# Three-layer fp32 kernel: mLSTM values and the joined local values and gates computed with tokens as the stationary operand

## Chip, cores and metric

One core of one Trainium2 chip runs the whole program. The metric is device time in microseconds (us) of one execution; a time given for a kernel is the median of its runs.

## The reference

The program is two layers of one kind and then one of another, on 512 tokens (S) of width 1024. In each of the first two layers a normalised x is projected, mixed by two branches, projected back and followed by an MLP:

```
h = rmsnorm(x, norm_mix_g[l]);  proj = h @ w_in
mqk, mv, mo, mi, mf, aq, ak, av, ga, gb = split(proj)   # widths 1024 1024 1024 4 4 1024 256 256 1024 1024
mq, mk = split(silu(causal_conv(mqk)));  mv: 4 heads of 256
hm = mlstm(mq, mk, mv, ig = mi + b, logf = log_sigmoid(mf + b))  # normalised, * sigmoid(mo)
ha = sliding_window_attention(aq, ak, av)                  # 16 query heads of 64, 4 key/value heads
x += (sigmoid(ga) * (hm @ w_branch_m) + sigmoid(gb) * (ha @ w_branch_a)) @ w_out
x += square(relu(rmsnorm(x) @ w_up)) @ w_down
```

The change touches `mv` (the mLSTM's values, four heads of 256), `av` (the window attention's "local" values, 256 wide) and the gates `mi`, `mf` (4 each). The third layer (an NSA layer with three attention branches and 48 gate columns) is touched only in how its gate weights are held.

## The kernel before

**Number format.** Every large product is made of three fp32r matmuls: high part by high part, low by high, high by low. ScalarE rounds a weight tile to its high part `w_hi`, GpSimd subtracts to get `w_lo`, and the activations have a high and a low part too: `hx` from x times the gain alone (not yet normalised), `hT` from the normalised x.

**Units.** Weights come in *units* of 128 output columns by 1024 inputs (512 KB), loaded by SP into a two-deep ring `w_raw`, split by ScalarE and GpSimd. A unit is 24 matmuls of 512 columns on TensorE, given in four quarters `u0 h0 m1 u1` of six (function `quarter`): the weights are the stationary operand, the 512 tokens move, and the result lies feature-major (features on partitions) in PSUM bank 0 or 1. A layer has 140 units. In all three layers TensorE's order is written out by hand as lists of steps, and every engine walks the same lists:

```
PRE_TAIL = unit("v", 0) + unit("v", 1) + [("TK", 0)] + CONV[0:2] + [("TK", 1)] + CONV[2:3] + [("gatesT",)]
PRE_FIRST = unit("k", 0) + unit("k", 1)[:3] + [("norm_",)] + unit("k", 1)[3:] + [("gates",)] + PRE_TAIL
loop_turn: [begin] + CONV[done:] + unit("conv", 1) + unit("mv", 0) + unit("mv", 1)
           + [("TV", 0)] + unit("q", 0) + [("TV", 1), ("bc",)] + unit("q", 1) + place_fill([("ST", 0), ...
```

**The stretch ahead of the loop (PRE).** Keys `k` come from `hx`, so TensorE can start before the norm is known. `norm_` sums the squares over partitions with a matmul against ones, ScalarE makes `rs` (the reciprocal root) of it (`norm`, L1191, L1193), and VectorE multiplies results by it later (`store`, L1676). `gates` (`gate_gemm`, L692 to L694) multiplies a full 128-column unit of gate weights, padded from 8 columns, with 24 matmuls of 512 columns. Then come two units of local values `v`; since attention wants them token-major, VectorE scales them into `vtmp` and TensorE transposes them in groups of four 128x128 tiles (`TK`, helper `heads4`, L681). Meanwhile VectorE makes the eight tiles of the normalised x (`tile`, L1802), ScalarE their high parts (L1224), VectorE their low parts (`tile_lo`, L1796), and VectorE and ScalarE work on four-partition rows of the gates (`gate_rows_in`, `gate_rows`, `gate_rows_max`, L1842 to L1857). `gatesT` (L739) transposes these rows. `conv 0` is the first unit on `hT`.

**The loop.** Four turns, one for each head. A turn has units conv 0 and 1 (queries and keys of the mLSTM head), `mv` 0 and 1 (its values), q 0 and 1, six gate units, and between their quarters the small matmuls of both attentions: `bc`, `ST` (scores), `NUM` (values times scores, with `vbuf` as the moving operand) and the window's steps. The `mv` result is feature-major as well: ScalarE copies it to `vtmp`, TensorE transposes it (`TV`, `heads4`), ScalarE copies it to `vbuf`.

**Elsewhere.** `head_values` (L653 to L655) already computes the third layer's values the other way: the 128x128 tile of tokens is stationary and 512 columns of weights move, so that the result comes token-major in four banks.

## Time and profile before

| | |
|---|---|
| median of 3 runs | 2216.64 us (2215.83 to 2217.93) |
| the profiled execution's own time | 2215.26 us |
| its span in the trace | 2213.5 us |
| instructions | 31354 |
| TensorE busy (matmuls) | 2170.8 us, 10211 matmuls |
| VectorE, ScalarE, GpSimd busy | 1047.5, 1085.4, 974.4 us |
| mean granted TensorE clock | 0.996 |
| DMA | 198.70 MB, mean 90 GB/s |

The busy times are sums of modelled durations with overlaps taken out. A matmul's record is longer than the distance to the next one, because successive matmuls are pipelined; what a matmul costs on TensorE is the distance between the starts of two neighbours.

### The profile page before, as it was taken

To read this page: it belongs to the slowest core of one execution; us is meant where nothing else is said; L and a number is where in the kernel's file an instruction comes from. 1 tells how busy PE (TensorE), PEld (TensorE's weight loads), DVE (VectorE), ACT (ScalarE), POOL (GpSimd) and SP (SyncE) were. 2 spreads that over 40 slices of the span, in tenths; PEclk is the share of its full clock that TensorE was granted. 3 is DMA by queue.
4 is the path that set the end of the run, shared out by engine and by line. 5 is a ranking of instruction groups with operands and counts; after the bars stand their busy time and mean duration, and the time that the engine had idled before them with its cause. 6 is when DMAs were issued, how large, how long until landed. Compare 5 with 4: busy or idle time off the path is not lost.

```text
span 2213.5 us, 31354 instructions
## 1 busy us (share of the span) xinstructions
PE 2170.8 (98%) x10211; PEld 1790.0 (81%) x10211; DVE 1047.5 (47%) x2197; ACT 1085.4 (49%) x2267; POOL 974.4 (44%) x757
## 2 busy tenths in 40 slices
PE   7999999999999999999999999999999999999998
PEld 6888888888888888888888788888888787778766
DVE  7356355533132234563563723322324736767773
ACT  6456466434232234464564724322324427787783
POOL 3333333444444444433333344544444435555544
PEclk9999999999999999999999999999999999999999
DMA  4222222223232222222222232322222431221203
GB/s 141 77 86 77 86 86 67 86 95 105 98 102 93 97 95 95 86 77 77 88 75 86 67 104 99 102 95 95 95 95 95 165 124 58 77 67 49 77 29 124
DMA packets 60287, 198.70 MB, mean 90 GB/s; under 512 B 6814, under 2 KB 13519, under 8 KB 59536
## 3 DMA queue, kind: packets, MB, share of 16 engines
q1 hardware_dynamic: 54128, 184.43, 25.4%
q10 hardware_dynamic: 6048, 12.84, 1.6%
q8 instruction: 64, 1.05, 0.2%
q14 instruction: 47, 0.39, 0.1%
HBM read 192.99 MB, written 4.26 MB: 89 GB/s over the span
## 4 chain that ended last, share of the span: by engine, by line
issue 57%; POOL 26%; PE 10%; DVE 5%; ACT 1%; POOLq 1%; DMA 0%; DVEq 0%; ACTq 0%
POOL w_lo L546 26%; PE ps L644 2%; PE ps L646 2%; PE ps L645 2%; DVE Pn L2268 1%; PE ps L1008 1%; PE ps L999 1%; PE ps L1021 1%; DVE PTn L2284 1%; POOLq L542 1%; PE ps L1022 1%; POOLq L544 1%; DVE ocur L2297 0%; DVE y L2255 0%; DVE sz L1733 0%
## 5 line engine op out<-in xcount | busy, mean ns | idle before, releaser
L546 POOL TENSOR_TENSOR w_lo<-w_raw,w_hi 128x512 fp32r<-128x512 f32 x592 | 780.8, 1326 | 1048.8 <-ACT w_hi L1088 1046.2
L644 PE MATMUL ps<-hT_hi,w_hi 128*128 128x512 f32 x1568 | 631.8, 403 | 1.7 <-DVE hT_lo L1796 1.1
L1088 ACT ACTIVATE w_hi<-w_raw 128x512 fp32r<-128x512 f32 x664 | 412.1, 627 | 421.6 <-PE ps L646 373.5
L646 PE MATMUL ps<-hT_hi,w_lo 128*128 128x512 f32 x1568 | 614.4, 392 | 0.0
L645 PE MATMUL ps<-hT_lo,w_hi 128*128 128x512 f32 x1568 | 613.4, 391 | 0.0
L646 PEld LDWEIGHTS ps<-hT_hi,w_lo 128*128 128x128 f32 x1568 | 295.5, 188 | 64.4
L644 PEld LDWEIGHTS ps<-hT_hi,w_hi 128*128 128x128 f32 x1568 | 296.0, 189 | 60.9 <-issue 2.4
L645 PEld LDWEIGHTS ps<-hT_lo,w_hi 128*128 128x128 f32 x1568 | 296.3, 189 | 56.4 <-issue 0.5
L644 PE MATMUL ps<-u_hi,w_hi 128*128 128x512 f32 x512 | 199.2, 389 | 0.0
L645 PE MATMUL ps<-u_lo,w_hi 128*128 128x512 f32 x512 | 199.2, 389 | 0.0
L646 PE MATMUL ps<-u_hi,w_lo 128*128 128x512 f32 x512 | 199.2, 389 | 0.0
L1768 DVE TENSOR_TENSOR x<-x,ps 128x512 f32<-128x512 f32 x64 | 44.0, 687 | 256.2 <-PE ps L646 256.2
L560 POOL TENSOR_TENSOR w_lo<-w_raw,w_hi 128x512 fp32r<-128x512 f32 x72 | 93.0, 1295 | 116.9 <-ACT w_hi L1088 116.9
L1740 DVE SCALAR_TENSOR_TENSOR e_buf<-ps,rs 128x512 f32<-128x512 f32 x64 | 44.3, 692 | 208.6 <-PE ps L646 208.6
L1141 ACT ACTIVATE u_hi<-e_buf 128x512 fp32r<-128x512 f32 x64 | 40.5, 633 | 172.9 <-DVE e_buf L1740 172.9
L644 PEld LDWEIGHTS ps<-u_hi,w_hi 128*128 128x128 f32 x512 | 96.1, 188 | 20.0
L646 PEld LDWEIGHTS ps<-u_hi,w_lo 128*128 128x128 f32 x512 | 96.1, 188 | 20.0
L645 PEld LDWEIGHTS ps<-u_lo,w_hi 128*128 128x128 f32 x512 | 96.1, 188 | 19.8
L1703 DVE SCALAR_TENSOR_TENSOR aq<-ps,aq 64x512 fp32r<-64x512 f32 x32 | 22.0, 689 | 149.7 <-ACT aq L1113 149.2
L1574 ACT ACTIVATE Pn<-Pn,st 128x128 f32<-128x128 f32 (+3 forms) x128 | 71.6, 560 | 25.2 <-DVE st L2268 25.1
L2268 DVE CUSTOM_DVE_ANT_0 Pn<-ps,biasn 128x128 f32<-128x128 f32 (+3 forms) x128 | 60.3, 489 | 24.9 <-DVEq L1649 24.5
L1392 ACT ACTIVATE Pw<-L,st 128x257 f32<-128x257 f32 (+1 forms) x128 | 60.9, 477 | 22.4 <-DVE st L2020 20.0
(339 smaller groups left out, 3489.7 us busy)
## 6 DMA issues: line engine op xcount, KB each, us to landing
w_raw<-w_all SPq DMA_DIRECT2D x332, 512.0 KB, 3.3
bias<-scr_w ACTq DMA_DIRECT2D x8, 512.0 KB, 3.7
biasn<-scr_n SPq DMA_DIRECT2D x4, 1024.0 KB, 5.7
w1k<-w_in ACTq DMA_DIRECT2D x2, 1024.0 KB, 7.2
w1v<-w_in ACTq DMA_DIRECT2D x1, 2048.0 KB, 12.6
scr_x<-x ACTq DMA_DIRECT2D x1, 2048.0 KB, 7.2
x<-scr_x SPq DMA_DIRECT2D x1, 2048.0 KB, 8.1
out<-x SPq DMA_DIRECT2D x16, 128.0 KB, 1.8
```

What stands on the lines that cost most here:

```text
L546: nc.gpsimd.tensor_tensor(w_lo[:, h, :], raw[:, h // 2, (h % 2) * HALF:(h % 2 + 1) * HALF], w_hi[:, h, :].bitcast(F32), ALU.subtract).then ...
L560: nc.gpsimd.tensor_tensor(w_lo[:, 2 * u.b + h, :], raw[:, u.b, h * HALF:(h + 1) * HALF], w_hi[:, 2 * u.b + h, :].bitcast(F32), ALU.subtrac ...
L644: nc.tensor.matmul(ps[:, p, :], wh, hi[:, kk, :], start=(kk == 0), stop=False)
L645: nc.tensor.matmul(ps[:, p, :], wh, lo[:, kk, :], start=False, stop=False)
L646: last = nc.tensor.matmul(ps[:, p, :], wl, hi[:, kk, :], start=False, stop=(kk == KT - 1))
L1088: nc.scalar.activation(w_hi[:, 2 * p + h, :], raw[:, p, h * HALF:(h + 1) * HALF], ACT.Copy)\
L1141: nc.scalar.activation(u_hl[0][:, n, :], e_buf[:, e.b, :], ACT.Square).then_inc(u_hi_done, 1)
L1392: nc.scalar.activation(Pw[:, qt % 2, hd, W0 - 1:W0 + n], L[:, hd, W0 - 1:W0 + n], ACT.Exp, scale=-1.0, bias=st[:, 0, j:j + 1], accum_out=s ...
L1574: nc.scalar.activation(p_, p_, ACT.Exp, scale=-1.0, bias=st[:, 0, j:j + 1], accum_out=st[:, 1, j:j + 1]).then_inc(probs, 1)
L1740: V.scalar_tensor_tensor(e_buf[:, e.b, :], g, 0.0, rs[:, :], ALU.max, ALU.mult).then_inc(g_free[u.b], 1)
L1768: V.tensor_tensor(x[:, n, :], x[:, n, :], g, ALU.add).then_inc(g_free[u.b], 1)
L2268: last = V.tensor_tensor_reduce(out=Pn[:, qt % 2, hd, 0:n], in0=ps[:, 2 + b_, e * n:(e + 1) * n], in1=reverse(biasn, hd, n), scale=1.0, sc ...
```

## The change

1. **Local values and gates together (`vg`).** The 256 columns of `av` and the 8 of the gates are one weight matrix of 264 columns (VW), in buffers of its own (`gv_hi`, `gv_lo`, `gv_raw`), loaded in two halves and split outside the ring. `group_values` computes them token-major: for each of the 8 input tiles k and 4 token tiles, the token tile of `hx` is stationary and 264 columns move. Results lie in four banks (2 to 5). ScalarE copies them out, scaled by the token's norm factor as a per-partition scalar (`group_out`). The units `v`, the product `gates` and the transposes `TK` go.
2. **The norm factor as a column.** Beside the matmul of `norm_`, step `norm0` has four matmuls of one column that give the sums token by token; two ScalarE instructions make `rs_tok` of them.
3. **The gate rows.** The gates are now token-major, so `GT` transposes them to rows (eight transposes of 128x4). VectorE's `gate_rows_in` has three instructions in place of four and comes behind all tiles of the normalised x.
4. **Values of heads 0 and 1 (`mx`).** Four units, in PRE, from `hx` (unnormalised), through `head_values`, token-major in banks 0 to 3; ScalarE scales by `rs_tok` on the way to two buffers `vbuf` (`first_pair_out`, eight copies).
5. **Values of heads 2 and 3 (`mv`).** Four units in turn 2 of the loop, from `hT`, the same way in banks 2 to 5 (`second_pair_out`). The other turns have no value units, and no turn has the transposes `TV`.
6. **Moves.** The tables' matmuls go between `mx` 1 and `mx` 2; `gatesT` between `mx` 2 and `mx` 3. The third layer's gate weights have 48 columns instead of 128. Units of a layer: 138.

The core of the diff:

```diff
-PRE_TAIL = (unit("v", 0) + unit("v", 1) + [("TK", 0)] + CONV[0:2] + [("TK", 1)] + CONV[2:3] + [("gatesT",)])
-PRE_FIRST = unit("k", 0) + unit("k", 1)[:3] + [("norm_",)] + unit("k", 1)[3:] + [("gates",)] + PRE_TAIL
-PRE_LATER = unit("k", 0)[:3] + [("norm_",)] + unit("k", 0)[3:] + [("gates",)] + unit("k", 1) + PRE_TAIL
+VALUES = [("vg", k) for k in range(KT)]
+PRE_FIRST = (unit("k", 0) + unit("k", 1)[:3] + [("norm0",)] + unit("k", 1)[3:] + VALUES + unit("mx", 0) + [("GT",)] + unit("mx", 1)
+             + [("tables",)] + unit("mx", 2) + [("gatesT",)] + unit("mx", 3) + CONV[0:3])
+PRE_LATER = (unit("k", 0)[:3] + [("norm0",)] + unit("k", 0)[3:] + unit("k", 1) + VALUES + unit("mx", 0) + [("GT",)] + unit("mx", 1)
+             + unit("mx", 2) + [("gatesT",)] + unit("mx", 3) + CONV[0:3])
...
-    return ([("begin",)] + CONV[done:] + unit("conv", 1) + unit("mv", 0) + unit("mv", 1)
-            + [("TV", 0)] + unit("q", 0) + [("TV", 1), ("bc",)] + unit("q", 1)
+    return ([("begin",)] + CONV[done:] + unit("conv", 1) + list(values) + unit("q", 0) + [("bc",)] + unit("q", 1)
...
+SECOND_PAIR = sum((unit("mv", n) for n in range(4)), [])
+LOOP = [loop_turn(CONV_BEFORE, WINDOW_NEXT, CONV_NEXT), loop_turn(CONV_NEXT, WINDOW_NEXT, CONV_NEXT),
+        loop_turn(CONV_NEXT, WINDOW_NEXT, CONV_NEXT, SECOND_PAIR), loop_turn(CONV_NEXT, WINDOW_END, 0)]
...
+            def group_values(l, k, sv, tv):
+                if k == 0:
+                    for b_ in range(2):
+                        pe.wait_ge(s_free[b_], sv[b_].m + 1)
+                        pe.wait_ge(t_free[b_], tv[b_].m + 1)
+                if k % 4 == 0:
+                    pe.wait_ge(gvlo_done, 2 * l + k // 4 + 1)
+                wh, wl = gv[0][:, k, 0:VW], gv[1][:, k, 0:VW]
+                for t in range(TT):
+                    last = token_products(ps[:, 2 + t, 0:VW], hx, k, t, wh, wl, k == 0, k == KT - 1)
+                    if k == KT - 1:
+                        last.then_inc((*s_ready, *t_ready)[t], 1)
...
+                    if s[0] == "norm0":
...
+                        nc.tensor.matmul(ps[:, 7, :], ones[:, :], ssq[:, :], start=True, stop=True).then_inc(o_ready[1], 1)
+                        for t in range(TT):
+                            last = nc.tensor.matmul(ps[:, 6, t:t + 1], ssq[:, t * P:(t + 1) * P], ones[:, 0:1], start=True, stop=True)
+                        last.then_inc(o_ready[0], 1)
...
+                        elif s == ("h0", "mx", 0):
+                            for b_ in range(2):
+                                pe.wait_ge(s_free[b_], cur["mx", "S"][b_].m + 1)
+                        head_values(s, cur["u"], hx, RAW_ORDER, (0, 1, 2, 3), (pair_ready, pair_ready, s_ready[0]))
...
+            def group_out(sv, tv):
...
+                    act.wait_ge(ready, use.m + 1)
+                    nc.scalar.activation(vtok[:, :, t, :], ps[:, 2 + t, 0:NG * DH].rearrange("p (g d) -> p g d", g=NG), ACT.Copy,
+                                         scale=rs_tok[:, t:t + 1])
+                    nc.scalar.activation(gtok[:, t, :], ps[:, 2 + t, NG * DH:VW], ACT.Copy, scale=rs_tok[:, t:t + 1]).then_inc(free, 1)
...
+            def pair_out(t, bank, scale=1.0):
+                nc.scalar.activation(vbuf[0][:, t, 0:MDV], ps[:, bank, 0:MDV], ACT.Copy, scale=scale)
+                return nc.scalar.activation(vbuf[1][:, t, 0:MDV], ps[:, bank, MDV:2 * MDV], ACT.Copy, scale=scale)
...
+                tile(l, 2, rs[:, :])
+                if l > 0:
+                    store(("u1", "k", 1), cur["k", 1])
+                for k in range(3, KT):
+                    tile(l, k, rs[:, :])
+                    tile_lo(l, k - 1)
+                tile_lo(l, KT - 1)
+                gate_rows_in(pre["GT",])
                 gate_rows()
...
+                gate_rows_max()
```

In layer 0's PRE, TensorE before the change (`hx` unnormalised x, `gw` gate weights, `vtmp` local values, `grow` gate rows, `hT` normalised x; one matmul of each kind of a repeated pattern is shown):

```order
L677 MATMUL ps<-ssq,ones 128x512
...
L692 MATMUL ps<-hx_hi,gw_hi 128x512
L693 MATMUL ps<-hx_lo,gw_hi 128x512
L694 MATMUL ps<-hx_hi,gw_lo 128x512
...
L700 MATMUL ps<-oh_w,tabw 16x384
L701 MATMUL ps<-oh_n,tabn 16x128
L704 MATMUL ps<-oh_n,tabn 16x256 x2
...
L681 MATMUL ps<-ident,vtmp 128x128 x4
L644 MATMUL ps<-hT_hi,w_hi 128x512
...
L739 MATMUL ps<-ident,grow 128x4 x8
```

And the same place in the changed kernel:

```order
L749 MATMUL ps<-ssq,ones 128x512
L751 MATMUL ps<-ones,ssq 128x1 x4
...
L668 MATMUL ps<-gv_hi,hx_hi 128x264
L669 MATMUL ps<-gv_hi,hx_lo 128x264
L670 MATMUL ps<-gv_lo,hx_hi 128x264
...
L668 MATMUL ps<-w_hi,hx_hi 128x512
...
L781 MATMUL ps<-ident,gtok 4x128 x8
...
L790 MATMUL ps<-ident,grow 128x4 x8
...
L659 MATMUL ps<-hT_hi,w_hi 128x512
```

The gate product and the transposes of `vtmp` are gone; 96 matmuls of 264 columns, four units of `mx`, four one-column matmuls and eight small transposes have come, and `gatesT` now has whole units on both sides.

ScalarE at the same place of the changed kernel, from the key copies to the second quarter of `mx` 0 (`st` holds `rs_tok`):

```order
L1252 ACTIVATE kdup<-kdup 64x512
L1271 ACTIVATE hT_hi<-ps 128x512 x6
L1278 ACTIVATE vtok<-ps,st 128x4x64
L1280 ACTIVATE gtok<-ps,st 128x8
...
L1145 ACTIVATE w_hi<-w_raw 128x512
L1271 ACTIVATE hT_hi<-ps 128x512
```

The copies of the joined product stand behind six of the eight high parts of the normalised x, where before they (of `vtmp`'s transposes, L1294 and L1295) stood between the last two.

## Rows read from the trace of the kernel before

**Rows 1.** Page, section 1: engine, busy us (share of the span), instructions.

```profile
PE 2170.8 (98%) x10211; PEld 1790.0 (81%) x10211; DVE 1047.5 (47%) x2197; ACT 1085.4 (49%) x2267; POOL 974.4 (44%) x757
```

**Rows 2.** Waits of PE, whole span: us in total, times, longest us.

```profile
PE ps L644 <- POOL w_lo L546: 9.9, 1, 9.9
...
PE ps L644 <- DVE hT_lo L1796: 1.1, 1, 1.1
```

**Rows 3.** Timeline of PE, gates product: start us, us, engine, line, operation.

```profile
23.39 0.39 PE L692 MATMUL ps<-hx_hi,gw_hi 128*128 128x512 f32 x1
...
28.85 0.39 PE L644 MATMUL ps<-hx_hi,w_hi 128*128 128x512 f32 x1
```

**Rows 4.** Groups of PE with shapes: count, busy us, mean ns.

```profile
L681 PE MATMUL ps<-ident,vtmp 128*128 128x128 f32 x80 | 12.0, 272 | 0.0
...
L653 PE MATMUL ps<-w_hi,hT_hi 128*128 128x512 f32 x32 | 12.4, 389 | 0.0
```

**Rows 5.** Timeline of PE, last layer's output in 256 columns.

```profile
2191.84 0.28 PE L1057 MATMUL ps<-y_hi,w_hi 128*128 128x256 f32 x1
...
2197.11 0.28 PE L1059 MATMUL ps<-y_hi,w_lo 128*128 128x256 f32 x1
```

**Rows 6.** Timeline of the weight loads at the same place.

```profile
2191.84 0.19 PEld L1058 LDWEIGHTS ps<-y_lo,w_hi 128*128 128x128 f32 x1
```

**Rows 7.** Timeline of PE around the first group of transposes.

```profile
41.59 0.40 PE L646 MATMUL ps<-hx_hi,w_lo 128*128 128x512 f32 x1
41.83 0.60 PE L681 MATMUL ps<-ident,vtmp 128*128 128x128 f32 x4
42.19 0.48 PE L644 MATMUL ps<-hT_hi,w_hi 128*128 128x512 f32 x1
42.50 0.40 PE L645 MATMUL ps<-hT_lo,w_hi 128*128 128x512 f32 x1
```

**Rows 8.** Timeline of PE: matmuls of few columns, layer 1 and layer 2.

```profile
904.41 1.94 PE L739 MATMUL ps<-ident,grow 4*128 4x4 f32 x16
906.28 0.50 PE L644 MATMUL ps<-hT_hi,w_hi 128*128 128x512 f32 x1
...
1762.34 2.08 PE L912 MATMUL ps<-ident,rows_n 16*128 16x16 f32 x31
1764.35 0.50 PE L644 MATMUL ps<-hT_hi,w_hi 128*128 128x512 f32 x1
```

**Rows 9.** Timeline of PE behind layer 0's gatesT.

```profile
50.58 0.70 PE L644 MATMUL ps<-hT_hi,w_hi 128*128 128x512 f32 x1
...
54.34 0.39 PE L644 MATMUL ps<-hT_hi,w_hi 128*128 128x512 f32 x1
```

**Rows 10.** Stretches: busy of PE, PEld, DVE, ACT, POOL; granted clock, DMA share, GB/s.

```profile
52.00:54.00 2.00, 2.00 (x6) 1.59 (x5) 0.47 (x1) 1.64 (x3) 0.00 (x0) 0.50 0.84 251
```

**Rows 11.** Timeline of VectorE: norm factor used, layer 1's gate rows, two tiles.

```profile
23.50 2.81 DVE L1676 TENSOR_TENSOR kdup<-ps,rs 64x512 f32<-64x512 f32 x4 [3.07 <-ACT rs L1193]
...
883.15 0.68 DVE L1842 TENSOR_TENSOR grow<-ps,rs 4x512 f32<-4x512 f32 x1 [0.84 <-PE ps L694]
...
885.58 0.74 DVE L1802 SCALAR_TENSOR_TENSOR ps<-x,vl,rs 128x512 f32<-128x512 f32 x1
...
893.88 0.68 DVE L1857 TENSOR_TENSOR grow<-grow 4x512 f32<-4x512 f32 x1
...
903.44 1.86 DVE L1802 SCALAR_TENSOR_TENSOR ps<-x,vl,rs 128x512 f32<-128x512 f32 x1
```

**Rows 12.** Timeline of GpSimd beside that last tile.

```profile
903.46 1.29 POOL L546 TENSOR_TENSOR w_lo<-w_raw,w_hi 128x512 fp32r<-128x512 f32 x1 [1.97 <-ACT w_hi L1088]
```

**Rows 13.** Timeline of VectorE in loop turn 1: behind unit conv 1.

```profile
144.94 0.81 DVE L1715 TENSOR_SCALAR cv<-ps,vcur 128x512 f32<-128x512 f32 x1 [0.88 <-PE ps L646]
...
148.80 0.69 DVE L1724 SCALAR_TENSOR_TENSOR mqk<-e_buf,cv 128x512 f32<-128x512 f32 x1 [0.70 <-ACT e_buf L1127]
162.99 1.41 DVE L1703 SCALAR_TENSOR_TENSOR aq<-ps,aq 64x512 fp32r<-64x512 f32 x2 [13.50 <-ACT aq L1113]
```

More of the change, by code:

```diff
@@ L56 @@
 WROW = W0 + 2 * P
+VW = 2 * P + 2 * MH
+GW = 3 * 16
+VS = 3 * P
+RAW_ORDER = tuple((k + 2) % KT for k in range(KT))
 def unit(kind, n):
@@ L179, in takes @@
     out = list(TAKES.get(step[0], []))
-    if step == ("u0", "vn", 0):
+    if step in (("vg", 0), ("u0", "mv", 0), ("u0", "vn", 0)):
         out += ["S", "S", "T", "T"]
+    if step == ("u0", "mx", 0):
+        out += ["S", "S"]
     if step[0] == "u1" and step[1] in E_KINDS:
@@ L721, in _ @@
                                 waits=waits and (lambda k: (waits[0], waits[1] + k + 1)))
[L722 removed]
+                    elif s[0] == "tables":
+                        tables(us)
+                    elif s[0] == "GT":
+                        if l == 0:
                             pe.wait_ge(cst_in, 16 * 5)
[L724 to L731 removed]
+                        for b_ in range(2):
+                            pe.wait_ge(s_free[b_], cur["vg", "S"][b_].m + 2)
+                            pe.wait_ge(t_free[b_], cur["vg", "T"][b_].m + 2)
+                        for n, t_ in enumerate(us):
+                            pe.wait_ge(t_free[t_.b], t_.m + 1)
+                            for t in range(TT):
+                                last = nc.tensor.transpose(ps[0:MH, 4 + t_.b, t * P:(t + 1) * P], gtok[:, t, n * MH:(n + 1) * MH], ident[:, :])
+                            last.then_inc(t_ready[t_.b], 1)
                     elif s[0] == "gatesT":
@@ new lines, in first_pair_out @@
+            def first_pair_out(u, sv):
+                for t in range(2):
+                    act.wait_ge(pair_ready, 2 * cur["l"] + t + 1)
+                    act.wait_ge(g_free[t], cur["mx", 2 + t].m + 1)
+                    pair_out(t, t, rs_tok[:, t:t + 1]).then_inc(g_free[t], 1)
+                act.wait_ge(s_ready[0], sv[0].m + 1)
+                pair_out(2, 2, rs_tok[:, 2:3]).then_inc(s_free[0], 1)
+                product(u)
+                act.sem_inc(s_ready[1], 1)
+                pair_out(3, 3, rs_tok[:, 3:4]).then_inc(s_free[1], 1)
@@ new lines, in second_pair_out @@
+            def second_pair_out(u, sv, tv):
+                for t, (ready, free, use) in enumerate(((s_ready[0], s_free[0], sv[0]), (s_ready[1], s_free[1], sv[1]),
+                                                        (t_ready[0], t_free[0], tv[0]), (t_ready[1], t_free[1], tv[1]))):
+                    if t == TT - 1:
+                        product(u)
+                        act.sem_inc(ready, 1)
+                    act.wait_ge(ready, use.m + 1)
+                    pair_out(t, 2 + t).then_inc(free, 1)
@@ L1318, in _ @@
                 act.wait_ge(k_copied, 4 * (l + 1))
+                for b_ in range(2):
+                    act.wait_ge(s_free[b_], cur["vg", "S"][b_].m + 2)
+                    act.wait_ge(t_free[b_], cur["vg", "T"][b_].m + 2)
                 act.wait_ge(h_ready, (l + 1) * KT)
@@ L1443, in _ @@
                 stored()
-                gate_weights(l + 1, *((gw_raw,) if l < DEPTH - 1 else (gwn_raw,)))
+                if l == DEPTH - 1:
+                    gate_weights()
+                else:
+                    for hf in range(2):
+                        ks = slice(4 * hf, 4 * hf + 4)
+                        nc.scalar.dma_start(gv_raw[:, ks, 0:VW], wv_all[l + 1, :, ks]).then_inc(gv_in[hf], 16)
                 norm()
@@ L1677, in store @@
                     last.then_inc(g_free[u.b], 1)
-                elif kind == "v" and cur["layer"]:
-                    product(u)
-                    V.tensor_tensor(vtmp[:, n, :], g, rs[:, :], ALU.mult).then_inc(g_free[u.b], 1)
                 elif kind == "k":
@@ L1880, in _ @@
                     pre[s] = take(s)
-                    if s == ("u1", "v", 0) and l == 0:
-                        for r in ("S", "S", "T", "T"):
-                            w.use(r)
                 if l > 0:
```

342 lines of the change are left out of this document (168 added, 174 removed).

## The prediction

> **What bounds the kernel now.** I read the busy shares first, then TensorE's waits, then its timeline. TensorE is busy 98% of the span, and no other engine half of it [rows 1]. Its waits are few: 9.9 us is the start, before the first weights are split, and in the stretch that the change rewrites one wait of 1.1 us for the last low parts of the normalised x stands out [rows 2]. So the time is TensorE's instruction stream, and a change is worth what it takes out of that stream, less any wait that it opens. A record's duration is no price, since records overlap: the 24 matmuls of the gates product have records of 0.39 us but take 28.85 - 23.39 = 5.46 us, 0.2275 us each [rows 3]. All prices below are such distances.
>
> **The change, part by part, for one layer.**
>
> *Removed.* The padded gates product: 5.46 us [rows 3]. The two units of local values: 48 x 0.2275 = 10.92 us. The transposes: two groups TK and eight TV. One group of four starts at 41.83, where the next unit's matmul would have started, and puts that unit's second matmul to 42.50 instead of 42.06: 0.44 us [rows 7]. Its start alone moves by 0.36 us, the lower bound. The trace counts 80 such matmuls in two layers, 20 groups [rows 4]. Ten groups are 4.4 us. Together 20.8 us.
>
> *Added.* The joined product has 8 x 4 x 3 = 96 matmuls of 264 columns, each with a weight load of its own. The nearest stream is the last layer's output in halves: from 2191.84 to 2197.11 lie 44 matmuls of 256 columns, with a 128x128 load each, 0.120 us apart [rows 5]. Between 256 columns at 0.120 and 512 at 0.2275 eight columns are worth 0.003, so 0.123 x 96 = 11.8 us. The four one-column fp32 matmuls of norm0: gatesT's eight fp32 matmuls in this layer stand as 16 instructions in the trace, two for each, and take 1.87 us, 0.117 us an instruction [rows 8]. Eight of them: 0.94 us; the 31 cheapest small ones of the trace, 2.01 us together [rows 8], would make it 0.5. I take 0.9, the row of the same type. GT has eight transposes with a stationary tile of only 4 columns: between 0.065 each (those 31) and 0.11 (a quarter of a TK group), 0.5 to 0.9 us; I take 0.75. Together 13.5 us.
>
> *Moved at no price.* The eight value units of a layer stay eight, with 192 matmuls of 512 columns; only the roles of the operands are exchanged. The kernel already does so in the third layer, and these matmuls have records of 389 ns, those of the ordinary ones [rows 3, 4]. The third layer's gate product keeps its 24 matmuls of 512 columns. Weight splitting: two units fewer for a layer in the ring, and the 264 columns are split by ScalarE (two instructions of about the size of the one before) and GpSimd in layer 0, by ScalarE and VectorE under the MLP in layer 1. Their cover at the start is the 11 us of units k; the load is about twice the bytes in SP's queue, behind the first two units and x, and is first needed at 24 us. Were that cover gone, vg would wait for GpSimd's split, about 2.5 us a half.
>
> *Waits.* The 1.1 us for the low parts goes: conv 0 now stands four units (22 us) behind the joined product, and the tiles no longer share VectorE with gate rows. Late next is the chain through ScalarE: mx 0's second quarter writes banks 2 and 3, and these come free when ScalarE has copied the joined product, behind six high parts of tiles. From the norm factor VectorE needs the four key products (2.81 us from 23.50 [rows 11]) and ten tile operations of about 0.7, to about 35 with half a microsecond for the later norm factor (two more ScalarE instructions, and the four small matmuls before them). The joined product ends at about 36.2 and the banks are asked for 1.4 us later. So there is about 1 us of slack, and tiles can eat it: one tile product takes 0.74 us, another 1.86 beside GpSimd's subtraction, which starts at the same moment [rows 11, 12]. Behind gatesT: the row work lasted from 883.15 to 894.56 in layer 1, 11.4 us with two other jobs in it [rows 11]; without them it is about 9, and GT to gatesT has two units, 10.9 us, so it holds, by 2 us. Queued behind the ScalarE wait for these rows are weight splits, which have two units of lead. I put 0.3 us a layer on new waits; bounds 0 and 1.5.
>
> *In the loop.* Turns 0, 1 and 3 lose 10.9 us of units between conv 1 and the scores. In turn 1 the queries and keys are ready at 149.5 us, 4.6 us behind conv 1's end, and VectorE then idles 13.5 us before the next job [rows 13]. Two q units, 10.9 us, still lie between. No wait.
>
> **The sum.** 20.8 - 13.5 = 7.3 us a layer, 14.5 in two (rounded once); plus 1.1 for the wait that goes, less 0.6 for new ones: 15.0 us. The profiled execution took 2215.26 us, so 2200.3; the median of the runs is 1.4 us above that execution, and against it the forecast is **2201.6 us**. A measurement of this kernel can tell about 0.2%, 4.4 us, from no change.
>
> **The clock.** Behind gatesT the granted clock falls to half: the stretch from 52 to 54 shows 0.50, that is 1.2 GHz [rows 10], and eight matmuls take 54.34 - 50.58 = 3.76 us in place of 1.82 [rows 9]. That is 1.9 us, and layer 1 does the same. The 31 small transposes of the third layer lasted as long and were followed at once by matmuls of 0.50 and shorter, with no fall [rows 8]. So a stretch of small matmuls may bring a fall or not. I keep two falls in the sum, for gatesT stays as it is.
>
> **Rivals.**
>
> *Falls vanish.* Before, gatesT followed shortly on TK groups and, in layer 0, the 1.1 us wait; now it has whole units on both sides. Without the two falls the gain is 15.0 + 3.8 = 18.8 us: 2197.8. Against it: layer 1 had no wait there and fell. The Trainium skill ("TensorE: Matmul & The Clock Gate", Part 4: PE-mode transpose) says that transposes do not count as busy for the clock as other matmuls do; by it, taking TK away ahead of gatesT speaks for this rival, and no run here has shown it alone. Chance 0.13.
>
> *More falls.* norm0 (a 512-column fp32 matmul and now 0.9 us of one-column ones) and GT are new stretches of low work. Two more falls give 15.0 - 3.8 = 11.2 us: 2205.4. Chance 0.14.
>
> *The weight loads set the pace.* A load's record is 0.19 us [rows 6], longer than 0.123. If loads did not overlap with these matmuls, 192 of them would cost 192 x (0.19 - 0.123) = 12.9 us more: gain 2.1 us, 2214.5, no visible change. Against it: the 256-column stream has the same records, 0.12 us apart [rows 5]. The Trainium skill ("TensorE: Matmul & The Clock Gate", Part 3: Packing small matmuls, The mechanism) lists weight loads as overlapping with running matmuls only when the row group differs, which full 128-row tiles never do; it would make this rival true. The trace disagrees, at 0.12 us. Chance 0.05, in which I count also that the new stream is slow for another reason.
>
> *Slower: the cover lost in the loop turns wants more than it gave.* The value units were also TensorE's filler while VectorE and ScalarE finish a turn and prepare the next. Six turns lose them. If the scores of each had to wait for the queries and keys, or the first quarters for banks, each wait above 15.0 / 6 = 2.5 us turns the gain into a loss; at 4 us each it is 9 us slower: 2225.6. For that the chain behind conv 1 would have to reach 10.9 + 4 us, against 4.6 measured [rows 13]. Chance 0.03.
>
> **How the numbers follow.** Forecast 0.65, falls vanish 0.13, more falls 0.14, loads 0.05, slower 0.03. Faster by over 0.2% are the first three, 0.92; within 0.2%: 0.05; slower 0.03. The range takes in the first three cases: 2197 at the low end (no falls, and the transposes and small matmuls at their better bounds), and 2207 at the high one (two more falls and a further microsecond and a half of waits).
>
> **What would show it.** Each step right: 96 matmuls of 264 columns a layer, 0.12 us apart; no wait on hT_lo at conv 0; TensorE's matmul count down by 24 + 48 + 40 and up by 96 + 8 + 8 instructions a layer; turns 0, 1 and 3 shorter by about 11.8 us, turn 2 longer by 10.0. Wrong: a wait of TensorE on ScalarE's `vtok`/`gtok` copies at mx 0 or on the row work at gatesT, waits at the scores of turns 0, 1 and 3, or 264-column matmuls 0.19 us apart. The clock row behind gatesT and norm0 decides between the first three cases.

## The result, and the profile after

| | kernel before | changed kernel |
|---|---|---|
| time, median (executions) | 2216.23 us (4) | **2196.38 us** (4), 2194.03 to 2197.65 |
| ratio, 95% interval | | 0.9911 (0.9899 to 0.9923) |
| profiled execution | 2215.26 us, span 2213.5 | 2197.65 us, span 2195.9 |
| pooled over three comparisons (and the base of experiments 4, 5 and 8), median, mean | 2215.2, 2215.1 us (76) | 2196.6, 2197.3 us (14) |

The change is faster, by 0.9%. The forecast of 2201.6 us had the sign and most of the size, but the result lies 5.2 us below it and 0.6 us below its range. The second and third comparison gave 0.9923 (0.9909 to 0.9936) and 0.9920 (0.9907 to 0.9934); in the end the base was 1.4 us lower than the three runs shown, and the gain 18.5 us by medians (17.8 by means) where 15.0 had been forecast. Two single executions, one of the kernel before (4420.61 us) and one of experiment 9's narrow kernel (4368.1 us), took about twice the time of all others, and no median below counts them.

The page of the changed kernel, section 1, answers to [rows 1]:

```profile
PE 2155.0 (98%) x10211; PEld 1777.0 (81%) x10211; DVE 1052.2 (48%) x2190; ACT 1077.8 (49%) x2273; POOL 965.8 (44%) x750
```

TensorE's count is that of before because the changes cancel (24 + 48 + 40 out, 96 + 8 + 8 in, a layer); its busy time is 15.8 us less. Its waits answer to [rows 2]:

```profile
PE ps L659 <- POOL w_lo L558: 9.0, 1, 9.0
PE ps L1056 <- DVEq L2352: 5.4, 16, 1.4
...
PE ps L659 <- DVE hx_lo L1887: 1.1, 2, 0.7
```

No row of this view names hT_lo, and none names vtok, gtok or the gate rows at unit mx 0 or at gatesT: the wait went, and no new one is large enough to be listed (one of 0.14 us is shown below). The 1.1 us on `hx_lo` lie at the start, ahead of norm0, and are absent in two further profiles of the same kernel (r1_after, r3_after). The new stream, in the timeline of TensorE (start us, us, engine, line, operation):

```profile
22.05 1.02 PE L749 MATMUL ps<-ssq,ones 128*128 128x512 f32 x2
22.91 0.95 PE L751 MATMUL ps<-ones,ssq 128*128 128x1 f32 x8
23.72 0.48 PE L659 MATMUL ps<-hx_hi,w_hi 128*128 128x512 f32 x1
...
25.19 0.28 PE L668 MATMUL ps<-gv_hi,hx_hi 128*128 128x264 f32 x1
25.31 0.28 PE L669 MATMUL ps<-gv_hi,hx_lo 128*128 128x264 f32 x1
...
36.59 0.28 PE L670 MATMUL ps<-gv_lo,hx_hi 128*128 128x264 f32 x1
36.71 0.39 PE L668 MATMUL ps<-w_hi,hx_hi 128*128 128x512 f32 x1
...
42.15 1.03 PE L781 MATMUL ps<-ident,gtok 128*4 128x128 f32 x8
42.94 0.47 PE L668 MATMUL ps<-w_hi,hx_hi 128*128 128x512 f32 x1
```

The 96 matmuls of 264 columns go from 25.19 to 36.71: 11.52 us, 0.120 each (forecast 0.123). The one-column ones take 23.72 - 22.91 = 0.81 us, and norm0's whole addition is 0.89 (forecast 0.9): from its first matmul through six more of the unit it was 2.25 us, it is 3.14. GT takes 0.79 us, and the unit behind it 5.64 in place of 5.44: 0.99 (forecast 0.75).

How near the waits were, in ScalarE's timeline and VectorE's:

```profile
35.89 0.60 ACT L1271 ACTIVATE hT_hi<-ps 128x512 fp32r<-128x512 f32 x1 [0.79 <-DVE ps L1899]
36.52 0.47 ACT L1278 ACTIVATE vtok<-ps,st 128x256 f32<-128x256 f32 x1
...
37.04 0.47 ACT L1278 ACTIVATE vtok<-ps,st 128x256 f32<-128x256 f32 x1
```

```profile
48.11 2.20 DVE L1948 TENSOR_TENSOR_SCAN grow<-grow 4x512 f32<-4x512 f32 x1
...
53.21 0.68 DVE L1954 TENSOR_TENSOR grow<-grow 4x512 f32<-4x512 f32 x1
```

ScalarE had copied bank after bank from 36.52 on, 0.5 us each. The second bank was free at 37.68 and the second quarter of mx 0 came at 38.07 without a wait: 0.4 us to spare, where 1 had been forecast. The gate rows were done at 53.89; gatesT asked for them at 56.12, 2.2 us later. That is the forecast's number, but not its reason: the row work took 9.8 us in place of 9, and layer 0 has the tables between GT and gatesT besides the two units. Layer 1 has no tables there, its row work took 10.9 us (891.78 to 902.67), and nothing was left. VectorE's last operation on the rows, and TensorE:

```profile
901.07 1.60 DVE L1954 TENSOR_TENSOR grow<-grow 4x512 f32<-4x512 f32 x1
```

```profile
902.26 0.39 PE L670 MATMUL ps<-w_lo,hx_hi 128*128 128x512 f32 x1
902.72 1.94 PE L790 MATMUL ps<-ident,grow 4*128 4x4 f32 x16
```

gatesT started 0.05 us behind the end of the rows and 0.46 us behind the start of the matmul ahead of it, where layer 0 has 0.32: a wait of 0.14 us, too short for the list of waits. r1_after and r3_after show the same 0.46. So the cover that the mx units give is used up in layer 1.

The loop turns, read at the one matmul with `negM` that each turn has; its starts were 76.45, 162.00, 247.01 and 332.00 before, and are now:

```profile
80.00 0.49 PE L819 MATMUL ps<-negM,selh 36*128 36x512 f32 x1
...
153.65 0.49 PE L819 MATMUL ps<-negM,selh 36*128 36x512 f32 x1
...
248.59 0.49 PE L819 MATMUL ps<-negM,selh 36*128 36x512 f32 x1
...
321.80 0.49 PE L819 MATMUL ps<-negM,selh 36*128 36x512 f32 x1
```

The three distances went from 85.55, 85.01 and 84.99 to 73.65, 94.94 and 73.21 us: 11.9 shorter, 9.9 longer, 11.8 shorter, where 11.8, 10.0 and 11.8 were forecast. No wait was opened in the loop. One and the same turn differs by 0.44 us from execution to execution in both kernels (73.21 or 73.65, 85.00 or 85.45), without a wait in the list; why is open.

**Falls of the clock.** What did not come as forecast is the clock behind gatesT [rows 9, 10]. In this execution there was no fall in either layer. The same place in two executions of the changed kernel, the one shown and another (run r3_after), as the stretch from 59 to 61 us (busy of PE, PEld, DVE, ACT, POOL; granted clock, DMA share, GB/s):

```profile
59.00:61.00 2.00, 2.00 (x10) 1.64 (x9) 0.39 (x3) 0.00 (x0) 0.00 (x0) 1.00 0.78 260
```

```profile
59.00:61.00 2.00, 2.00 (x7) 1.54 (x6) 0.00 (x0) 0.00 (x0) 0.00 (x0) 0.50 0.55 215
```

The count in brackets takes in every matmul with a part in the 2 us: ten at 1.00 (2.4 GHz), seven at 0.50 (1.2 GHz). The same kernel, the same instructions ahead of it.

### The profile page after: what moved, and what is told of

It reads as the page before. It is cut to its first block, busy times and chain, and to the rows that moved or that the text cites. A ratio compares the mean times of both kernels' runs of the same rounds, so it can differ in the third digit from the quotient of the medians.

```text
span 2195.9 us, 31306 instructions
## 1 busy us (share of the span) xinstructions
PE 2155.0 (98%) x10211; PEld 1777.0 (81%) x10211; DVE 1052.2 (48%) x2190; ACT 1077.8 (49%) x2273; POOL 965.8 (44%) x750
## 4 chain that ended last, share of the span: by engine, by line
issue 56%; POOL 26%; PE 9%; DVE 5%; ACT 1%; POOLq 1%; DMA 0%; DVEq 0%; SPq 0%; ACTq 0%
POOL w_lo L558 26%; PE ps L659 2%; PE ps L661 2%; PE ps L660 2%; DVE Pn L2348 1%; PE ps L1065 1%; PE ps L1056 1%; PE ps L1078 1%; PE ps L1079 1%; DVE PTn L2364 1%; POOLq L554 1%; POOLq L556 1%; DVE y L2335 0%; DVE ocur L2377 0%; DVE sz L1830 0%
## 5 line engine op out<-in xcount | busy, mean ns | idle before, releaser
L558 POOL TENSOR_TENSOR w_lo<-w_raw,w_hi 128x512 fp32r<-128x512 f32 x584 | 769.7, 1325 | 1038.9 <-ACT w_hi L1145 1036.6
L1145 ACT ACTIVATE w_hi<-w_raw 128x512 fp32r<-128x512 f32 x656 | 406.7, 626 | 440.1 <-PE ps L661 358.6
L659 PE MATMUL ps<-hT_hi,w_hi 128*128 128x512 f32 x1440 | 579.9, 403 | 0.4 <-DVE x2v L1790 0.4
L661 PE MATMUL ps<-hT_hi,w_lo 128*128 128x512 f32 x1440 | 563.4, 391 | 0.0
L660 PE MATMUL ps<-hT_lo,w_hi 128*128 128x512 f32 x1440 | 562.7, 391 | 0.0
L661 PEld LDWEIGHTS ps<-hT_hi,w_lo 128*128 128x128 f32 x1440 | 271.0, 188 | 59.3
L659 PEld LDWEIGHTS ps<-hT_hi,w_hi 128*128 128x128 f32 x1440 | 271.5, 189 | 54.5 <-issue 2.4
L660 PEld LDWEIGHTS ps<-hT_lo,w_hi 128*128 128x128 f32 x1440 | 271.8, 189 | 51.7 <-issue 0.5
L569 POOL TENSOR_TENSOR w_lo<-w_raw,w_hi 128x512 fp32r<-128x512 f32 x72 | 93.1, 1296 | 116.4 <-ACT w_hi L1145 116.4
L659 PE MATMUL ps<-y_hi,w_hi 128*128 128x512 f32 x176 | 68.7, 390 | 1.7 <-DVE y_lo L2387 1.7
```

Source lines behind the costliest of these rows:

```text
L558: nc.gpsimd.tensor_tensor(w_lo[:, h, :], raw[:, h // 2, (h % 2) * HALF:(h % 2 + 1) * HALF], w_hi[:, h, :].bitcast(F32), ALU.subtract).then ...
L569: nc.gpsimd.tensor_tensor(w_lo[:, 2 * u.b + h, :], raw[:, u.b, h * HALF:(h + 1) * HALF], w_hi[:, 2 * u.b + h, :].bitcast(F32), ALU.subtrac ...
L659: nc.tensor.matmul(ps[:, p, :], wh, hi[:, kk, :], start=(kk == 0), stop=False)
L660: nc.tensor.matmul(ps[:, p, :], wh, lo[:, kk, :], start=False, stop=False)
L661: last = nc.tensor.matmul(ps[:, p, :], wl, hi[:, kk, :], start=False, stop=(kk == KT - 1))
L1145: nc.scalar.activation(w_hi[:, 2 * p + h, :], raw[:, p, h * HALF:(h + 1) * HALF], ACT.Copy)\
```

## The experiments

A short name for the stretches used below: **layer 0** and **layer 1** are the distance from the first matmul of the norm (`norm_` before, norm0 now) to that layer's first matmul on `hm`, which is where the loop ends and the branches are projected, ahead of the MLP; **third** is from the last layer's first matmul of `hx` to the last matmul. All times in us; "fall" is a fall of the clock directly behind gatesT; in brackets stands how many falls the third layer had anywhere. The last two kernels of each half belong to experiment 9 and differ from the others only in the third layer's gate product.

| profiled execution | layer 0 | layer 1 | third (falls) |
|---|---|---|---|
| before (shown) | 368.94, fall | 370.09, fall | 478.42 (2) |
| r1_before | 368.80, fall | 368.80 | 478.43 (2) |
| r3_before | 367.78 | 370.44, fall | 477.88 (1) |
| r4_third_gate_narrow_a | 370.79, fall of twice the length | 370.58, fall | 478.33 (2) |
| r4_third_gate_narrow_b | 369.36, fall | 368.98 | 477.75 (1) |
| after (shown) | 357.94 | 361.83 | 479.23 (3) |
| r1_after | 359.59, fall | 362.29 | 479.32 (3) |
| r3_after | 359.09, fall | 362.96, fall | 479.27 (3) |
| r4_third_gate_wide_a | 358.86 | 361.39 | 479.25 (3) |
| r4_third_gate_wide_b | 359.60, fall | 360.86 | 478.25 (2) |

The start, from the first instruction to the norm's first matmul, took 20.5 to 22.8 us in the five profiles of the first half and 21.0 to 22.2 in the second, 21.7 on average in both. What lies in neither the start nor these columns agrees within 0.1 us. So the ten profiles account for their whole time: on average the spans are 2213.6 and 2196.5 us, 17.1 apart, and layer 0 gives 10.1 of it, layer 1 7.9, the third layer takes 0.9 back.

**1. Both kernels again, twice.** No edit.

> The kernel before, once more, for its spread and a second profile. Theory A (the instruction stream lost 14.5 us and a wait of 1.1 us, and the two falls of the granted clock behind gatesT, 1.9 us each, went with the change): about 2216 us, and this profile shows both falls again, each behind gatesT of layers 0 and 1. Theory B (the stream alone lost 19 to 20 us, and the clock falls come and go by chance): the falls move or are absent in this profile.

> The changed kernel, once more. Theory A: 2195 to 2198 us, and no clock fall behind gatesT in either layer; from norm0 of a layer to the first hm matmul 358 us in layer 0 and 362 us in layer 1, as in the first profile. Theory B: falls appear in one of the two places now and then, so this profile differs from the first by 1.9 us or more in a layer.

> The kernel before, once more. Its own spread is what it is for. In two profiles of it so far a fall of the clock stood behind gatesT of layer 0 both times, of layer 1 once. If falls come by chance, a third profile may show another pattern; the times should lie at 2213 to 2218 us.

> The changed kernel, once more. Theory A (the part of the gain that does not depend on falls is 15 to 16 us, the rest is a fall or two that did not come): 2196 to 2200 us, ratio 0.991 to 0.993, and a norm-to-MLP stretch of layer 0 of 357.9 us without a fall or 359.6 with one. Theory B (the forecast's, two falls of 1.9 us kept in every run): a fall behind gatesT in both layers and a time of about 2200 to 2201 us.

Measured: before 2215.49 and 2215.64, changed 2198.99 (2196.11 to 2199.81) and 2196.27 (2196.08 to 2199.45). The table shows what the spread is made of. Falls behind gatesT come and go from execution to execution in both kernels. With the fall in layer 0 the stretch to the first turn's `negM` matmul lasts 55.31 us in the kernel before, without it 53.70; in the changed one 59.54 and 57.95. So a fall costs 1.6 us (the forecast had 1.9). Theory B of the last expectation, a fall in both layers in every run, is out. Like compared with like (one fall against one, none against none, means over the table, the long fall left out), layer 0 became 9.5 us shorter and layer 1 7.3. The third layer, 478.2 to 479.1 on average, became 0.9 longer.

What the falls do to the whole can be read from all executions, since the mean granted clock of each is on record. Over 88 of the kernel before and 14 of the changed kernel it is 0.9963 in both (one record of 0.946, at a usual time, is left out). Executions at the same clock differ by the same amount: at 0.996 the means are 2215.49 (49) and 2197.83 (9), 17.7 us apart, at 0.997 they are 2213.90 (32) and 2196.13 (3), 17.8 apart. So the gain of 17.8 us does not come from fewer falls. Fewer behind gatesT and one more in the third layer cancel.

**2. Token-major values alone.** From the kernel before: the head values are made token-major in two turns of the loop, and TV goes; the padded gates product and TK stay. The edit, cut:

```diff
-            + [("TV", 0)] + unit("q", 0) + [("TV", 1), ("bc",)] + unit("q", 1)
+PAIR = sum((unit("mv", n) for n in range(4)), [])
+LOOP = [loop_turn(CONV_BEFORE, WINDOW_NEXT, CONV_NEXT, PAIR), loop_turn(CONV_NEXT, WINDOW_NEXT, CONV_NEXT),
+        loop_turn(CONV_NEXT, WINDOW_NEXT, CONV_NEXT, PAIR), loop_turn(CONV_NEXT, WINDOW_END, 0)]
...
+                            head_values(s, cur["u"], hT, range(KT), (2, 3, 4, 5), (s_ready[0], s_ready[1], t_ready[0]))
```

> The kernel before with one part alone: the values of all four heads token-major, four units in turn 0 and four in turn 2, both from the normalised x; gates, local values, their transposes and gatesT stay. 16 groups of four transposes go. Theory A: 16 x 0.44 = 7.0 us less than before, about 2209 us, with the falls behind gatesT still there. Rival (cover lost in the turns without value units): waits at the scores or at the pair's banks, and less than 4 us gained. Theory B: 10 us or more.

Measured: 2209.76 (2207.33 to 2212.84), ratio 0.9977 (0.9968 to 0.9986), 5.4 us below before and 10.8 above the changed kernel of the same comparison. So some 30% of the gain comes with the token-major head values, and the rest with the joined product and the values taken from unnormalised x. The falls behind gatesT that were expected still did not come in this profile, in neither layer. In this kernel the part from `hm` to the next `hx` took 482.27 us in each layer in place of 481.08, without a wait, most of it lost in the first 86 us. Some of its buffers lie 128 bytes further on than in the kernel before; whether this is the reason was not tried, and it stays open.

**3. Transposes back.** In the changed kernel, eight groups of four transposes a layer of the identity, results unused, two in each turn:

```diff
+                            if s[0] == "u0" and s[1] == "q":
+                                pe.wait_ge(g_free[us[0].b], us[0].m + 1)
+                                for t in range(TT):
+                                    nc.tensor.transpose(ps[:, us[0].b, t * P:(t + 1) * P], ident[:, :], ident[:, :])
```

> The changed kernel with a group of four transposes of the identity put back ahead of each q unit of the two layers, 16 groups, written to a PSUM bank that the unit overwrites. Theory A: 16 x 0.44 = 7.0 us more than the changed kernel, about 2203.4 us, no new clock fall. Theory B: more than 9 us.

Measured: 2204.67 (2203.78 to 2206.17) for 16 groups, 5.7 us above the changed kernel's 2198.99 in the same comparison, 8.1 above its pooled 2196.6: medians of five are too coarse for a price. In the profiles, fall against fall: layer 0 362.44 against 359.59 and 359.09, layer 1 366.28 against 362.96. That is 0.36 to 0.42 us a group. A turn of two groups took 74.03 us where the shorter of the two usual lengths is 73.21: 0.41 a group, between the forecast's bounds of 0.36 and 0.44.

**4. Transposes right ahead of gatesT.** The Trainium skill ("TensorE: Matmul & The Clock Gate", Part 4: PE-mode transpose) says that transposes do not count as busy for the clock in the way of other matmuls. By it, two groups of them ahead of gatesT make the stretch of low work longer, and a fall more likely:

```diff
+                            if which == 0:
+                                for o_ in us:
+                                    pe.wait_ge(t_free[o_.b], o_.m + 1)
+                                    for t in range(TT):
+                                        nc.tensor.transpose(ps[:, 4 + o_.b, t * P:(t + 1) * P], ident[:, :], ident[:, :])
```

> The changed kernel with two groups of four transposes of the identity right ahead of gatesT in each layer, into the banks that gatesT then overwrites. If transposes close ahead of gatesT made the clock fall (the kernel before had such groups 3 and 6 us ahead of it): 4 x 0.4 = 1.6 us for the transposes and 3.8 us for two falls, together 5.4 us more than the changed kernel, about 2201.8, with the granted clock at 0.5 behind gatesT. If what matters is whole units on both sides: 1.6 us more, about 2198, no fall.

Measured: 2197.67 (2196.69 to 2199.69), and in its profile no fall behind gatesT in either layer (358.84 and 362.44). Ahead of gatesT (1.9 us) eight transposes took 1.0 us, and they do not bring the fall by themselves. The run does not bear the rule out; and where half of the layers fall anyway, two layers without a fall don't refute it.

**5. gatesT twice.** Its eight fp32 matmuls issued two times over (`for t in (*range(TT), *range(TT))`).

> The changed kernel with each of gatesT's small matmuls done twice: 16 more instructions of 0.117 us in each layer, 1.9 us a layer. If the length of a stretch of small matmuls decides on the fall: 3.8 us for the matmuls and 3.8 us for two falls, about 2204. If not: 3.8 us more, about 2200.2.

Measured: 2203.67 (2201.76 to 2206.03). Falls in both layers; in layer 0 (363.38) the clock fell within gatesT, which took 4.51 us, and ten slow matmuls followed instead of seven; in layer 1 364.67. Of the 7 us above the changed kernel, 3.6 are the matmuls themselves (gatesT of layer 1 takes 3.66 us in place of 1.87); most of the rest are the two falls.

**6. gatesT in four parts.** Two matmuls ahead of each quarter of unit mx 3:

```diff
+                        if s[1:] == ("mx", 3) and s[0] != "u0":
+                            gates_turned(late, ts[s[0]])
...
-                        for which in range(2):
+                        for t_ in us:
...
+                        gates_turned(us, range(0, 2))
```

> The 8 small fp32 matmuls of gatesT are issued 2, 2, 2 and 2, ahead of the four quarters of unit mx 3, in place of all 8 (1.9 us) ahead of the first. Nothing is left out. Theory A (a fall behind gatesT comes from one unbroken stretch of small matmuls): no fall at gatesT in either layer; each of the three new interruptions costs what restarts do, about 0.1 us, so 0.3 us a layer; stretch of layer 1 at 362.1 to 362.6 us, of layer 0 at 358.2 to 358.8, whole time within 1 us of the changed kernel. Theory B (falls have nothing to do with how these matmuls lie together): a fall in layer 0 in about every second execution still, 1.6 us more there.

Its timeline at layer 0's gatesT:

```profile
54.87 0.60 PE L746 MATMUL ps<-ident,grow 4*128 4x4 f32 x4
55.40 0.50 PE L668 MATMUL ps<-w_hi,hx_hi 128*128 128x512 f32 x1
...
56.99 0.60 PE L746 MATMUL ps<-ident,grow 4*128 4x4 f32 x4
57.52 0.50 PE L668 MATMUL ps<-w_hi,hx_hi 128*128 128x512 f32 x1
```

Measured: 2198.73 (2196.4 to 2200.3), no faster than the changed kernel. A part takes 0.53 us and the six matmuls behind it 1.59 in place of 1.37. From norm0 to the first `negM` it is 59.10 us in place of 57.94 in layer 0 and 62.62 in place of 61.44 in layer 1, so the four parts cost 1.2 us a layer more than one piece, where 0.3 had been expected. There was no fall in either layer, but two profiled layers of one kind are too few: the changed kernel too had none in three of its six. Doubling (5) and splitting go the way of theory A, the length of the unbroken stretch of small matmuls, but two layers each show no more than a hint.

**7. norm0's one-column matmuls twice.**

> The four one-column fp32 matmuls of norm0 are done twice in each layer, 8 instructions more. The forecast priced 8 such instructions at 0.9 us and feared falls behind norm0. Theory A (they cost 0.1 us each, the trace of the changed kernel has 0.81 us for 8, and bring no fall): 0.8 us a layer, 1.6 in all, 2198 to 2201 us, norm0's one-column stretch 1.6 us long. Theory B (a longer stretch of small work, 2.5 us with the 512-column fp32 matmul, makes the clock fall behind norm0): matmuls 0.43 us apart behind it and 1.5 us more a layer, about 2201 to 2204 us.

```profile
22.24 1.02 PE L749 MATMUL ps<-ssq,ones 128*128 128x512 f32 x2
23.10 1.84 PE L751 MATMUL ps<-ones,ssq 128*128 128x1 f32 x16
24.80 0.48 PE L659 MATMUL ps<-hx_hi,w_hi 128*128 128x512 f32 x1
```

Measured: 2199.68 (2199.29 to 2202.22). 16 instructions take 1.70 us, eight more cost 0.89, and no fall follows. The rival "more falls" at norm0 has no support: with 2.6 us of small work there it did not happen.

**8. First head pair's values in turn 0**, from normalised x as in turn 2. This takes the four mx units from between the joined product, GT, gatesT and conv 0 (ScalarE's last high parts of the normalised x then stand right behind its copies of the joined product):

```diff
-             VALUES + unit("mx", 0) + [("GT",)] + unit("mx", 1)
-             + [("tables",)] + unit("mx", 2) + [("gatesT",)] + unit("mx", 3) + CONV[0:3])
+             VALUES + [("GT",)]
+             + [("tables",)] + [("gatesT",)] + CONV[0:3])
...
-LOOP = [loop_turn(CONV_BEFORE, WINDOW_NEXT, CONV_NEXT), 
+LOOP = [loop_turn(CONV_BEFORE, WINDOW_NEXT, CONV_NEXT, SECOND_PAIR), 
```

> The changed kernel with one part undone: the values of heads 0 and 1 are computed in turn 0 of the loop from the normalised x, as those of heads 2 and 3 are in turn 2, so that nothing lies between the joined product and GT, the tables, gatesT and conv 0. The matmuls are the same in number. If the four units ahead of the loop are cover for the gate rows and the tiles of the normalised x: GT waits for ScalarE's copies (about 2.5 us), gatesT for the row work (about 9 us, less 1.9 of tables in layer 0), 20 to 23 us in two layers, and perhaps clock falls behind the idle stretch (3.8 us): 2217 to 2223 us, the whole gain gone. If the row work were short or hidden otherwise: under 5 us more.

Measured: 2220.38 (2219.09 to 2221.59), ratio 1.0026 (1.0017 to 1.0035): slower than the kernel before. TensorE's waits in it:

```profile
PE ps L790 <- DVE grow L1951: 11.6, 2, 8.0
...
PE ps L781 <- ACT gtok L1276: 3.2, 2, 1.8
...
PE ps L731 <- DVE grow L1937: 1.9, 1, 1.9
```

These 16.7 us of waits are what the cover saves that the first two heads' values from unnormalised x give, the part of the change that looks like a mere move. A second cost comes with them. Where TensorE waits so much (7.2 us in layer 0, 9.4 in layer 1) the granted clock goes to 0.50 and stays there past gatesT: in layer 0 from 41.72 to 55.37 and in layer 1 from 901.88 to 915.53 us. A stretch within the first (as above), and gatesT:

```profile
44.00:46.00 2.00, 0.11 (x1) 0.00 (x0) 1.93 (x3) 0.59 (x1) 0.00 (x0) 0.50 0.05 12
```

```profile
47.67 3.57 PE L790 MATMUL ps<-ident,grow 4*128 4x4 f32 x16 [3.56 <-DVE grow L1951]
51.17 0.80 PE L659 MATMUL ps<-hT_hi,w_hi 128*128 128x512 f32 x1
```

gatesT takes 3.50 us in both layers in place of 1.87, and ten matmuls behind it are 0.43 us apart: an estimate from these rows is 3.6 us a layer, and 0.9 for the tables. Without the cover the whole gain is gone.

**9. The third layer.** It became 0.9 us longer, and with a fall behind its 31 small transposes [rows 8] that the kernel before did not have. Other falls lie further back in this layer, in both kernels, at places that change from execution to execution. In the stretch from the gate product on, one thing differs that the forecast had passed over: the gate product's stationary tile is now 48 columns wide, before it was padded to 128. It was made wide in the changed kernel and narrow in the kernel before. The second, cut:

```diff
-                    wh, wl = gw[0][:, k * P:(k + 1) * P], gw[1][:, k * P:(k + 1) * P]
+                    W = 48 if I == DEPTH else P
+                    wh, wl = gw[0][:, k * P:k * P + W], gw[1][:, k * P:k * P + W]
```

> The changed kernel with the stationary tile of the third layer's gate product 128 columns wide again (48 wanted ones and 80 whose results nobody reads; two small extra copies on ScalarE and VectorE). Theory A (the narrow tile lets the clock fall behind the 31 small transposes that follow): no fall there, matmuls behind them 0.23 us apart, third layer at 477.9 to 478.4 us in place of 479.3, time 1 us below the changed kernel's 2196 to 2199. Theory B (chance, or the place in time): a fall there still, third layer at 479.3.

> The kernel before with the stationary tile of the third layer's gate product 48 columns wide (the padding is left out, results the same). Theory A: a fall behind the 31 small transposes, third layer at about 479.3 us in place of 478.4, time 1 us above before. Theory B: no fall there, as in all three profiles of before, and 478.4.

Each was profiled a second time, in the runs r4_third_gate_wide_b and r4_third_gate_narrow_b. Measured: wide 2197.39 (2196.36 to 2198.32), narrow 2216.01 (2212.88 to 2219.09). Behind the transposes the wide kernel fell in one profile of two (third 479.25 and 478.25), the narrow one in neither (478.33 and 477.75). The narrow one's timeline:

```profile
1766.33 2.08 PE L913 MATMUL ps<-ident,rows_n 16*128 16x16 f32 x31
...
1768.34 0.50 PE L644 MATMUL ps<-hT_hi,w_hi 128*128 128x512 f32 x1
...
1769.83 0.39 PE L644 MATMUL ps<-hT_hi,w_hi 128*128 128x512 f32 x1
1770.06 0.39 PE L645 MATMUL ps<-hT_lo,w_hi 128*128 128x512 f32 x1
```

and the wide one's:

```profile
1744.51 2.08 PE L969 MATMUL ps<-ident,rows_n 16*128 16x16 f32 x31
1746.52 0.50 PE L659 MATMUL ps<-hT_hi,w_hi 128*128 128x512 f32 x1
...
1747.98 0.63 PE L661 MATMUL ps<-hT_hi,w_lo 128*128 128x512 f32 x1
1748.41 0.63 PE L659 MATMUL ps<-hT_hi,w_hi 128*128 128x512 f32 x1
```

Starts 0.23 us apart in the one, 0.43 in the other, and the slow ones are the wide kernel's. Theory A is wrong: width does not decide. What stays is a count. Behind these transposes the clock fell in all eight profiles of the changed kernel and of its variants in 3 to 7, and in one of two of the wide kernel; it fell in none of five of the kernel before and its narrow variant. The kernel of 2, made from the kernel before, fell too, and that of 8 did not. The layer's length goes with the number of its falls wherever they are: 477.75 and 477.88 with one, 478.25 to 478.43 with two, 479.23 to 479.32 with three (table). What in the order or the time ahead of the transposes sets the odds is open.

## Why the forecast was off

The forecast was 2216.6 less 15.0. Against means of all executions its 5.2 us are 1.5 of base, 2.8 of gain, and 0.9 of luck, by which the four executions of the result lie below the mean of the fourteen.

*The base.* The three runs shown had a median of 2216.64, where the 76 have a mean of 2215.1. The result's own four changed executions are few as well: the second comparison's median, 2198.99, and the mean of the fourteen, 2197.3, both lie inside the range that the result missed by 0.6. That the result fell outside and not inside is luck of the draw; that it lies far from the middle is not.

*The step that failed: the term for the waits.* The sum has "plus 1.1 for the wait that goes, less 0.6 for new ones", 0.5 us together. It was worth 1.6. The 1.1 is the row of the list of waits for hT_lo. Around that wait the kernel before shows:

```profile
45.40 0.48 PE L644 MATMUL ps<-hT_hi,w_hi 128*128 128x512 f32 x1
...
47.49 0.50 PE L644 MATMUL ps<-hT_hi,w_hi 128*128 128x512 f32 x1 [1.14 <-DVE hT_lo L1796]
...
48.38 1.05 PE L739 MATMUL ps<-ident,grow 4*128 4x4 f32 x8
49.60 1.05 PE L739 MATMUL ps<-ident,grow 4*128 4x4 f32 x8 [0.17 <-ACT vtok L1295]
```

and in layer 1, without the wait:

```profile
902.84 0.48 PE L644 MATMUL ps<-hT_hi,w_hi 128*128 128x512 f32 x1
```

The six matmuls from 45.40 to gatesT took 2.98 us, those from 902.84 to 904.41 took 1.57 [rows 8]: 1.41 for the pause and the restart behind it. And gatesT itself was cut by a second wait, for ScalarE's copy of TK: 2.20 us (48.38 to 50.58) in place of 1.87. Together 1.74, where 1.1 was put. Of the 0.6 us for new waits 0.14 came, in layer 1.

*The other terms.* Like against like the two layers gave 9.5 + 7.3 = 16.8 us, 1.8 more than the 15.0. The waits are 1.1 of it. The joined product took 11.52 in place of 11.8 in each layer (0.6 for both), GT 0.99 in place of 0.75 (0.5 back), norm0 0.89 (0.9); a transpose group was 0.41 (0.44). The three turn distances together became 13.9 us shorter in layer 0 and 13.3 in layer 1 on average over the table's profiles (13.6). The units of values came at no price. Some 0.6 us stay unassigned.

*The clock: wrong as a mechanism, small in the sum.* "I keep two falls in the sum, for gatesT stays as it is." The profile of before showed a fall in both layers, and I took one execution's falls for a property of the kernel. Behind an unchanged gatesT the clock fell in 7 of 12 layers of the kernel before and its variants (experiments 2 and 9), and in 7 of 16 of the changed kernel and its variants (3, 4, 7 and 9), each worth 1.6 us, one of them twice that. So the kernel before has them not always, and the changed one not never; "falls vanish" as a certain mechanism is as wrong as "kept". In the ten profiles of the table the falls behind gatesT give 1.2 us of gain, and the third layer, whose falls the forecast did not count, takes 0.9 back. 7 of 12 against 7 of 16 can't say that the change alters the odds, and over all executions the granted clock is the same (experiment 1). The price of a fall was also misread: from 50.58 to 54.34 [rows 9] there are nine matmuls and not eight, so 3.76 us stand against 2.05 and not 1.82, and the fall is 1.6 to 1.7 us and not 1.9.

Sum: 15.0 + 1.8 (like against like) + 1.2 - 0.9 (falls) = 17.1 us, the difference of the ten spans. All executions together gave 17.8; the 0.7 between them has no cause that was found, and lies within what means over five profiles and over fourteen executions can differ: executions of one kernel spread over 6 us.

*The chain to the banks* was said to end at about 35 with 1 us of slack. Its terms as written add up to 33.8; the sixth high part ended at 36.49, and the slack was 0.4 us. That the gate rows would hold by 2 us came true in layer 0 through the tables and failed in layer 1. Both are near misses that cost nothing or 0.14 us here.

*The range* ended at 2197, and reached that only with no fall and the other small costs at their best. The spread between executions, bounds of tenths added up over two layers and a base from three runs should each have had a place at the low end.

*The rivals.* Weight loads: out, 0.120 us a matmul with a 128x128 load each. The Trainium skill ("TensorE: Matmul & The Clock Gate", Part 3: Packing small matmuls, The mechanism) lists weight loads as overlapping with running matmuls only where the row group differs; the 11.52 us of these 96 full-height matmuls are against it. Slower by lost cover in the turns: out, not one wait; yet experiment 8 shows that lost cover does turn this change into a loss, 16.7 us of waits and some 8 of low clock, in another place, ahead of the loop.

## What to carry to other kernels

Price a stream of matmuls by the distance of their starts in the trace, and count a pause by what the stretch around it lost against the same stretch without it: the list of waits gave 1.1 us for what was worth 1.7, and left out one of 0.14. When matmuls are taken out, look for the units that cover another engine's chain and move them there; here such a move, with no matmul less, was worth 24 us, more than the whole change. Check the slack in every layer: 2.2 us in one was nothing in the next. A clock fall seen in one profile is one draw: take two or three profiles of the kernel before as its base, give falls a share in the range and not a fixed term, and compare executions at the same mean granted clock.

## What was not expected of the hardware

- The clock's falls differ from execution to execution of one kernel. Behind an unbroken 1.9 us of small fp32 matmuls the clock fell in 14 of 28 profiled layers, behind 0.81 or 1.70 us of one-column ones in none. A fall is mostly seven matmuls, 0.427 us apart in place of 0.2275, and costs 1.6 us. What decides between two executions was not found.
- Small fp32 matmuls cost 0.10 us an instruction with one column and 0.117 with four, the 31 transposes of 16x16 0.065. An interruption of the stream by even four such instructions makes the next six matmuls 0.22 us longer (1.59 in place of 1.37).
- A 128x264 matmul with its own 128x128 load goes as fast as one of 256 columns, 0.120 us.
- Where TensorE waited 7.2 and 9.4 us around gatesT, the clock was at 0.50 for 13.65 us in each layer (experiment 8): the small matmuls of gatesT took 3.50 us in place of 1.87.
- Two kernels with the same matmuls behind the loop differed there by 1.2 us in 481 without any wait (experiment 2), for a reason that was not found.
